# A ring of six experts, and slot rows read in neighbouring blocks, in a two-layer hybrid decoder step

## What is computed

```
def hier_moe(x, w_coarse, b_coarse, w_fine, b_fine, w_gate, w_up, w_down):
    ...
    g_top, g_idx = lax.top_k(p_group, 1)
    ...
    e_top, e_idx = lax.top_k(p_exp, TOP_K_FINE)          # 2 of the group's 8
    ...
    h = jax.nn.silu(jnp.einsum('nd,edf->nef', xt, w_gate)) * jnp.einsum('nd,edf->nef', xt, w_up)
    y = jnp.einsum('nef,efd->nd', h * comb[:, :, None], w_down)
```

## Time and profile before

| what | us |
|---|---|
| median of 3 runs | 1709.87 |
| lowest, highest | 1708.14, 1718.1 |
| the profiled execution | 1702.48 |
| its span in the trace | 1700.8 |
| PE busy | 1243.0 (73%) |
| DVE busy | 501.1 (29%) |
| ACT busy | 332.2 (20%) |
| POOL busy | 189.5 (11%) |
| HBM traffic | 337 MB, mean 198 GB/s |

### The profile page before, as it was taken

One profiled execution on the slowest core, in us unless ns is written; L12 is line 12 of the kernel. 1 busy time (PEld: TensorE's weight loads), 2 busy tenths in 40 slices (PEclk: granted clock), 3 DMA queues, 4 the chain that ended last, 5 costly groups with the idle time before them and its releaser, 6 DMA issues. The chain is left out here.

```text
span 1700.8 us, 16762 instructions
## 1 busy us (share of the span) xinstructions
PE 1243.0 (73%) x6380; PEld 772.4 (45%) x6380; DVE 501.1 (29%) x1014; ACT 332.2 (20%) x572; POOL 189.5 (11%) x221
## 2 busy tenths in 40 slices
PE   1998958947777776189996588888799487666660
PEld 0676634424443333168885345444444344333330
DVE  1288853221111111300002233337722211111114
ACT  1324323110000000200001233337611100000001
POOL 0546520010000000200000100000000100000002
PEclk8799979968888888589999798979999688888885
DMA  6112704169999997332234355420041799999974
GB/s 149 45 50 73 299 6 149 50 240 351 359 361 357 361 367 277 106 87 74 74 106 167 140 196 190 158 99 1 1 148 50 245 368 363 365 358 359 362 253 171
DMA packets 234989, 337.52 MB, mean 198 GB/s; under 512 B 18882, under 2 KB 190914, under 8 KB 234904
## 3 DMA queue, kind: packets, MB, share of 16 engines
q1 hardware_dynamic: 213832, 301.65, 52.1%
q0 software_dynamic: 10112, 34.61, 5.4%
q10 hardware_dynamic: 10976, 0.33, 0.4%
HBM read 295.55 MB, written 41.87 MB: 198 GB/s over the span
## 5 line engine op out<-in xcount | busy, mean ns | idle before, releaser
L650 PE MATMUL psum<-arena 128*64 128x256 f32 x2048 | 288.6, 451 | 146.2 <-DMA arena<-moe_w_up 143.1
L650 PEld LDWEIGHTS psum<-arena 128*64 128x64 f32 x2048 | 175.4, 165 | 271.3 <-DMA arena<-moe_w_up 166.5
L1177 PE MATMUL psum<-arena 128*128 128x272 f32 x768 | 179.3, 397 | 5.9 <-DMA arena<-sb_w_qkv 5.9
L1177 PEld LDWEIGHTS psum<-arena 128*128 128x128 f32 x768 | 147.9, 193 | 37.3 <-issue 6.3
L732 PE MATMUL psum<-arena 128*128 128x512 f32 (+1 forms) x320 | 142.3, 600 | 9.0 <-ACT arena L577 7.9
L969 DVE TENSOR_TENSOR arena<-arena,psum 128x256 f32<-128x256 f32 x32 | 13.5, 421 | 412.7 <-PE psum L650 412.7
L667 PE MATMUL psum<-arena 128*64 128x512 f32 x512 | 116.9, 597 | 19.5 <-DVE arena L973 19.5
L404 PE MATMUL psum<-arena 128*128 128x272 f32 x512 | 121.6, 397 | 9.1 <-ACT arena L467 8.1
L404 PEld LDWEIGHTS psum<-arena 128*128 128x128 f32 x512 | 97.9, 192 | 34.5 <-issue 14.9
L719 POOL DMA_DIRECT2D slots_out<-arena x64 | 34.2, 538 | 607.3 <-DVE arena L979 607.3
L523 DVE SCALAR_TENSOR_TENSOR psum<-arena,vec,psum 128x512 f32<-128x512 f32 x138 | 92.9, 749 | 8.5 <-PE psum L414 8.4
(11 more groups left out here) (228 smaller groups left out, 1262.7 us busy)
## 6 DMA issues: line engine op xcount, KB each, us to landing
arena<-moe_w_gate SPq DMA_DIRECT2D x64, 1024.0 KB, 12.0
arena<-moe_w_up SPq DMA_DIRECT2D x64, 1024.0 KB, 12.3
arena<-moe_w_down SPq DMA_DIRECT2D x64, 1024.0 KB, 12.0
arena<-slots_in SPq DMA_DIRECT2D x64, 256.0 KB, 8.6
slots_out<-arena POOLq DMA_DIRECT2D x64, 256.0 KB, 7.8
arena<-cache_k SPq DMA_DIRECT2D x32, 512.0 KB, 5.7
arena<-cache_v SPq DMA_DIRECT2D x32, 512.0 KB, 5.2
arena<-sb_w_qkv SPq DMA_DIRECT2D x24, 512.0 KB, 3.6
```

The lines of the kernel that those rows point to most:

```text
L650: last = mat(K.ps[m][half[q], 0:FE], xe[:, k, q, :], (wg, wu)[m][u][:, k, :], start=(k == 0), stop=(k == KT - 1))
L1177: last = nc.tensor.matmul(K.ps[2 * u + n][:, 0:HALF], wt[u][:, k, :], HT[:, k, n * HALF:(n + 1) * HALF], start=(k == 0), stop=(k == KT - 1))
```

## The change

The row number of a slot becomes expert times 64 plus rank (MAIN rows in all), so that the 64 rows of an expert, and the 128 of a pair, are neighbours in HBM. A slot beyond 64 goes to a separate area behind them: `place` adds a `jump` where the rank is 64 or more. With that, rows of a pair are read by one DMA of 128 rows into 128 partitions, and stored by one.

The buffers of the loop (`xe`, `yo`, `gs`, `h`, `hT`, `xr`) move over the normalised rows at A_HN, and `xr` has two instead of three. The ring grows to six experts and reaches down over the conv output and the routing's temporaries. Pair 0 takes its slots 2 and 3, pair 1 slots 4 and 5, pair 2 slots 0 and 1, which lie over what the routing uses; so SP loads pair 2 after DVE signals `late`, behind its last routing instruction. The row reads go from SP's queue to ACT's: the first two after the scatter, that of pair g + 2 ahead of the Silu of pair g.

```diff
-RING = 4
+RING = 6
...
+SLOT0 = (2, 4, 0)
...
             weights(0)
             weights_down(0)
             sp.wait_ge(s["y"], 2 * NB)
             weights(1)
             weights_down(1)
-            sp.wait_ge(s["scattered"], 16 * 2 * NB)
-            for g in range(3):
-                rows_in(g)
-            for g in range(PAIRS - 2):
+            sp.wait_ge(s["late"], 1)
+            weights(2)
+            weights_down(2)
+            for g in range(PAIRS - 3):
                 sp.wait_ge(s["up"], g + 1)
-                weights(g + 2)
-                if g + 3 < PAIRS:
-                    rows_in(g + 3)
+                weights(g + 3)
                 sp.wait_ge(s["out"], g + 1)
-                weights_down(g + 2)
+                weights_down(g + 3)
...
-                for q in range(2):
-                    pool.dma_start(ys_rows[2 * g + q, 0:CAP, :], yo[g % 2][half[q], :]).then_inc(s_store[g % 2], 16)
+                pool.dma_start(K.ys_dram[P * g:P * g + P, :], yo[g % 2]).then_inc(s_store[g % 2], 16)
...
+            def rows_in(g):
+                act.dma_start(xr[g % 2], K.xs_dram[P * g:P * g + P, :]).then_inc(s_rows[g % 2], 16)
+
+            act.wait_ge(s["scattered"], 16 * 2 * NB)
+            rows_in(0)
+            rows_in(1)
             for g in range(PAIRS):
                 v = g % 2
                 act.wait_ge(s["gate"], g + 1)
+                if g + 2 < PAIRS:
+                    act.wait_ge(s["turned"], g + 1)
+                    rows_in(g + 2)
...
+                v.tensor_scalar(jump[x, b, :], ef[x, b, :], float(FAR - CAP), float(MAIN - CAP), ALU.mult, ALU.add)
...
-                v.scalar_tensor_tensor(out=K.pos[x, b, :], in0=rank[x, b, :], scalar=float(NE), in1=ef[x, b, :], op0=ALU.mult, op1=ALU.add).then_inc(s["pos"], 1)
+                v.scalar_tensor_tensor(out=slot[x, b, :], in0=ef[x, b, :], scalar=float(CAP), in1=rank[x, b, :], op0=ALU.mult, op1=ALU.add)
+                do(v.scalar_tensor_tensor(out=jump[x, b, :], in0=rank[x, b, :], scalar=float(CAP), in1=jump[x, b, :], op0=ALU.is_ge, op1=ALU.mult))
+                do(v.tensor_tensor(slot[x, b, :], slot[x, b, :], jump[x, b, :], ALU.add))
+                v.tensor_copy(K.pos[x, b, :], slot[x, b, :]).then_inc(s["pos"], 1)
...
+            dve.sem_inc(s["late"], 1)
```

More of the change, by code:

```diff
@@ L170, in conv_layout @@
     K.conv_end = at
-    K.w2 = K.region(A_RING + 2 * EW, KT, D)
-    K.conv_b2 = K.region(A_END - D, D)
-    K.zero_rows = K.region(A_END - 3 * D, D)
+    K.w2 = K.region(A_END - KT * D, KT, D)
+    at = A_END - KT * D - 3 * D
+    K.conv_b2, K.zero_rows, K.conv_rows = (K.region(at + i * D, D) for i in range(3))
     K.s_zero = K.sem("slots_zeroed")
@@ L190, in stage_setup @@
     conv_layout(K)
-    rows = K.region(A_END - 2 * D, D)
+    rows = K.conv_rows
     hist = K.region(K.conv_end, 2, D)
@@ L596, in stage_moe @@
              "pos", "scattered", "chain", "wr", "prep", "exp", "gate", "up", "silu", "h", "ht", "hT", "turned", "xe",
-             "out", "ya", "yv")
+             "out", "ya", "yv", "late")
     s = {n: K.sem(L + n) for n in names}
@@ L600, in stage_moe @@
     K.s_wdown = [K.sem(f"{L}wdown{v}") for v in range(RING // 2)]
-    s_rows = [K.sem(f"{L}rows{i}") for i in range(3)]
+    s_rows = [K.sem(f"{L}rows{i}") for i in range(2)]
     s_store = [K.sem(f"{L}store{v}") for v in range(2)]
@@ L633, in stage_moe @@
     gs, h, hT = (K.region(at + i * FE, FE) for i in range(3)); at += 3 * FE
-    xr = [K.region(at + v * D, D) for v in range(3)]; at += 3 * D
-    assert at <= A_PREP
+    xr = [K.region(at + v * D, D) for v in range(2)]; at += 2 * D
+    assert at <= A_RING
     wg, wu, wd = [], [], []
@@ L977, in _ @@
                 if g >= 2:
-                    dve.wait_ge(s_store[p], 32 * (g // 2))
+                    dve.wait_ge(s_store[p], 16 * (g // 2))
                 v.tensor_copy(yo[p][:, 512:D], K.ps[5 + 2 * p][:]).then_inc(s["yv"], 1)
-    names = ("in", "turned", "xe", "gate", "up", "silu", "h", "ht", "hT", "y", "ya", "yv", "store", "stored", "w", "zero", "far", "ready", "back", "sum")
+    names = ("in", "turned", "xe", "gate", "up", "silu", "h", "ht", "hT", "y", "ya", "yv", "store", "stored", "w", "zero", "far", "ready", "back", "sum", "hn")
     r = {n: K.sem(f"{L}all_{n}") for n in names}
-    turns = EROWS // P
+    turns = FAR // P
+    again = K.region(A_RING + 2 * EW, NB, D)
     Y = K.region(A_HN, NB, 2, D)
@@ L995, in _ @@
                     for c in range(turns):
[L996 removed]
+                        n = turns * e + c
+                        sp.wait_ge(r["turned"], n + 1)
                         K.settle(sp)
[L998 removed]
+                        sp.dma_start(xr[0], K.xs_dram[bass.ds(P * n + MAIN, P), :]).then_inc(r["in"], 16)
         @block.tensor
@@ L1027, in _ @@
                 act.sem_inc(r["ya"], 1)
+                for b, rr in enumerate(ROWS):
+                    nc.scalar.activation(again[0:rr, b, :], K.X[0:rr, b, :], ACT.Copy, scale=K.rstd[0:rr, b:b + 1]).then_inc(r["hn"], 1)
                 with act.Fori(0, NE * turns) as n:
@@ L1097, in _ @@
                 for j in range(2):
-                    pool.indirect_dma_start(Y[0:rr, b, j, :], None, K.ys_dram[0:NE * CAP], bass.IndirectOffsetOnAxis(ap=K.near[0:rr, b, j:j + 1], axis=0)).then_inc(s_g[b], 16)
+                    pool.indirect_dma_start(Y[0:rr, b, j, :], None, K.ys_dram[0:MAIN], bass.IndirectOffsetOnAxis(ap=K.near[0:rr, b, j:j + 1], axis=0)).then_inc(s_g[b], 16)
         @block.scalar
         def _(act):
-            square_sums(K, act, s_c, 2, [K.region(A_RING + D * b, D) for b in range(NB)])
+            square_sums(K, act, s_c, 2, [K.region(A_RING + 2 * EW + D * b, D) for b in range(NB)])
         @block.vector
```

80 lines of the change are left out of this document (38 added, 42 removed).

## The result

| | before | after |
|---|---|---|
| median of four runs, us | 1712.42 | 1661.54 |
| lowest, highest | 1708.14, 1718.10 | 1659.92, 1663.44 |
| span of the profiled execution | 1700.8 | 1660.6 |
| PE's idle time ahead of gate and up, ended by moe_w_up | 143.1 | 106.4 |

The ratio is 0.970 (95% interval 0.967 to 0.974): 51 us faster, where the forecast was 62. The time lies inside the range and 13.5 us above the predicted number. That the sum came out near is partly luck: two of its terms were wrong, in opposite directions.

What follows compares the result with a forecast made beforehand. The weight stream bounds the expert loops. Per layer it falls from 283 to 249.5 us; less a 3 us hole, plus 0.5 at the tail, 31 are saved, 62 in all: 1648 us on the median's footing, range 1628 to 1678.

Steps and rivals of the forecast that it cites:

- third pair ahead, less the hole: Idle stream from 366 to 384 gets pair 2's weights: 16.2 us a layer, less a 3 us hole before pair 3.
- rows in 128 partitions, less the extra read: Thirteen loop row reads at 400 GB/s save 18.7 us a layer; one more read in the full stretch costs 1.3.
- stores in 128 partitions: After the last pair POOL issues one DMA instead of two: 0.5 us per layer.
- What bounds it: In the expert loops the weight stream is the bound; TensorE's waits ahead of gate and up end with moe_w_up landing.
- thirteen reads at 193 GB/s cost 2.72 us each: Price of slots_in row reads in the loop before; at 400 GB/s they were to take 1.31 us, 1.41 less.
- I count nothing in the stream: Stores already ran at 391 GB/s beside another queue, so no gain there; bounds 0 and 0.1 us each.
- Gate and up at 387: Rate in GB/s for the loop's gate and up weights in 1 KB pieces, read from the earlier trace.
- ACT's issue: ACT issuing a row DMA ahead of each Silu costs nothing: 2.05 us against 3.1 us free.
- Rival 3: ACT's issue blocks while SP's queue is backed up; slower from about 12 us an issue, 1758 us at 14; chance 3%.
- Rival 1: Row reads stay slow for a reason the change keeps, so only the prefetch counts: 1688 us; chance 10%.
- rival 2: Prefetch eaten at the start: first rows starve or scatter slows, up of pair 0 8 to 16 us later; 1658 to 1674; 12%.
- rival 4: Nothing moves: three queues in one stretch cost the stream the whole 31 us a layer; 1710 us; chance 3%.

Runs made afterwards that it cites:

- e7: Kernel after without the third pair loaded ahead, SyncE loading pair g+2 when up of pair g is done; 1694.6 us, ratio 0.987.
- e9: Kernel before with each pair's two 64-partition row DMAs joined into one of 128, the 64 ranks outermost, same SyncE queue; 1662.7 us, ratio 0.972.
- e12: Kernel after with each store of a pair's result cut into two DMAs of 64 partitions; 1666.6 us, ratio 0.973.
- e1: Kernel after with its ring moved 128 bytes towards the front, so slots begin at multiples of 256 bytes; 1630.5 us, ratio 0.950.
- e4: Kernel before with its ring moved 128 bytes towards the front, so slots begin 128 bytes beside a multiple of 256; 1760 us, ratio 1.026.
- e5: Kernel after with each read of a pair's rows cut into two DMAs of 64 partitions, still neighbouring rows on ScalarE; 1705.7 us, ratio 0.991.
- e8: Kernel after with rows issued by SyncE in the weights' queue, behind the weights of later pairs, instead of by ScalarE; 1725.8 us, ratio 1.004.
- e6: Kernel before with each pair's two row DMAs joined into one of 128 partitions, the 2 experts outermost; 2016.6 us, ratio 1.173.
- e2: e1 with the pair loop's buffers also moved 32 floats back, so row reads and stores begin at multiples of 256 bytes; 1633.6 us, ratio 0.953.

## Why the prediction was right, and where it was not

Per layer, from loop times (the two layers as a pair):

| term | forecast | measured | by |
|---|---|---|---|
| third pair ahead, less the hole | 16.2 - 3 = 13.2 | 13.8, 13.8 | e7 |
| rows in 128 partitions, less the extra read | 18.7 - 1.3 = 17.4 | 21.8, 24.1 | e9 (on before, no extra read) |
| stores in 128 partitions | 0.5 | 2.6, 2.9 | e12 |
| sum | 31 | 38.2, 40.8 | |
| the same, measured at once | | 38.9, 40.7 | e1 |
| address of the ring | not seen | -17.0, -16.7 | after less e1 |
| the change | 31 | 21.9, 24.1 | after |

That the loss is the address is shown by e1 and e4. The three terms, taken one at a time, add up to what e1 shows for all at once within 1 us, so I see no sign of another term of size. But they come from different kernels, and the extra read is in none of them: on the kernel after, with its slower stream, e5 gives the rows only 14.8 and 17.4 a layer, and why it is less I have not shown. The total came within the range because the three terms together gained 7 to 10 us a layer more than forecast while the address lost 17; that the two offset each other is luck.

- **What bounds it**: right; PE still waits for moe_w_up, and every run moved with the stream.
- **Third pair**: right in size. "up" of pair 0 came 3.45 us later (376.64 + 9.46 = 386.10, before 382.65); I took 3.
- **Rows**: right cause (e5, e9), wrong size. The step that failed is "thirteen reads at 193 GB/s cost 2.72 us each": a rate read at the bottom of a dip times the bytes of one transfer. The window of 193 GB/s was not of rows alone either: 74 of its 165 pieces were under 2 KB. The dip was 4.75 us long and cost 2.0 us instead of 1.41. What remains open is whether the 64 partitions or the cut into two DMAs is slow, since each run changed both. The section of the Trainium skill's page "SBUF — State Buffer" that the prediction cites speaks for the partitions; so do the two w_down DMAs of a pair, which follow one another with 128 partitions each at 159 ns a piece in e1.
- **Stores**: the step "I count nothing in the stream" held (e12); the tail's 0.5 us, the second issue alone, left out that a store in halves is slower when nothing runs beside it (10.6 us to the gather instead of 8.0).
- **The stream's rate**: the step that failed most. "Gate and up at 387", carried over from the earlier trace rows, assumed that a moved slot streams as before. Six places of 24576 bytes counted back from A_END end up half a line off, and gate and up run at 350. The diff showed A_RING change; I did not work out the address.
- **ACT's issue**: right; a read takes 0.33 us to issue, in the median of 32, far below the 3.1 us that were free. Rival 3 did not happen.
- **Rival 1** fell with the rows' pieces in after (171 ns, in e5 261) and with e9, **rival 2** with the full windows of after, **rival 4** with the result. Without the queue (e8) the time is the one that rival 4 had.

## What to carry to other kernels

When a change moves a buffer that DMAs fill with short runs, work out its byte address in the partition before anything else: half a 256-byte line cost a tenth of the rate of the 1 KB pieces here, and 17 us a layer, more than the 13.8 that the third pair brought. Price a slow transfer by the whole stretch in which the rate is low, against the rate beside it, and not by its bytes at the lowest rate. And before joining DMAs, look at the outermost run of the pattern (2 left the DMA on two engines in e6, 64 did not in e9), and ask of a queue which order it allows, at the end of the loop too.

## What the runs showed of the hardware

- A 1 KB piece written 128 bytes off a 256-byte line took 50.9 ns instead of 46.1 (after, e1); a 4 KB piece of rows took 159 either way (e1, e2). With the ring off its line, the row pieces of another queue took 171 instead of 159 (after, e1).
- One DMA whose outermost run is 2 ran, by its share of 0.12 to 0.15, on two engines of 16, at 49 to 58 GB/s (e6).
- An issue by ACT took 0.33 us in the median, at most 0.45, in the same loops of after in which SP's issues took up to 8.2 us (7.7 from 440 to 600): the backlog of one queue did not hold up the other.
- Stores of 64 partitions cost next to nothing beside a full stream, and 2.6 us at the end, alone (e12).
